# A Hymba decoder layer on one Trainium2 core: the two widest score levels with 66 stationary columns, and one mean square for both value tiles of a GLA head

## The reference

```python
def step(S, inp):                       # per chunk of a head
    q_, k_, v_, g_ = inp
    b = jnp.cumsum(g_, axis=-2)
    diff = b[..., :, None, :] - b[..., None, :, :]
    decay = jnp.exp(jnp.where(causal, diff, -jnp.inf))
    A = jnp.einsum('bhid,bhjd,bhijd->bhij', q_, k_, decay)
    o_intra = jnp.einsum('bhij,bhje->bhie', A, v_)
    o_inter = jnp.einsum('bhid,bhde->bhie', q_ * jnp.exp(b), S)
...
def head_rmsnorm(o, g):                 # over the dv values of a head: 256 in GLA, 128 in HGRN2
    y = o32 * lax.rsqrt(jnp.mean(o32 * o32, axis=-1, keepdims=True) + EPS)
```

## Time and profile before

| | |
|---|---|
| median of three runs | 916.29 us (915.92 to 916.40) |
| the profiled execution | 916.32 us |
| its span in the profile | 914.60 us |
| PE busy | 899.2 us, 98% of the span |
| PEld busy | 746.9 us, 82% |
| DVE busy | 524.7 us, 57% |
| ACT busy | 396.1 us, 43% |
| score matmuls, all levels (L499) | 576 records, 64.5 us of matmul |

### The profile page before, as it was taken

How to read it: one execution, slowest core, us unless ns; L and a number is a source line. 1 busy time by engine, 2 the same in 40 slices (tenths; PEclk the granted TensorE clock), 3 DMA queues, 4 the chain that set the end, 5 groups by cost and what they waited for, 6 DMA issues and landing times.

```text
span 914.6 us, 12106 instructions
## 1 busy us (share of the span) xinstructions
PE 899.2 (98%) x4451; PEld 746.9 (82%) x4451; DVE 524.7 (57%) x838; ACT 396.1 (43%) x536; POOL 64.9 (7%) x95
## 2 busy tenths in 40 slices
PE   8999999999999999999999999999999999999995
PEld 5787888888888888888888888888888888888884
DVE  6632442226365373643457777786875669555756
ACT  6521522224252542525335444644654555434544
POOL 6000001111111100101111100000000000000000
PEclk9999999999999999999999999999999999999998
DMA  7252266667786754646985532123222536865654
GB/s 262 70 160 71 70 173 195 187 198 155 151 161 150 155 157 138 183 138 162 190 191 135 132 95 84 50 69 92 70 70 65 174 107 216 317 224 185 195 173 185
DMA packets 57557, 136.08 MB, mean 149 GB/s; under 512 B 6117, under 2 KB 6153, under 8 KB 56361
## 3 DMA queue, kind: packets, MB, share of 16 engines
q1 hardware_dynamic: 44050, 101.73, 36.0%
q0 software_dynamic: 11264, 33.56, 17.1%
q10 hardware_dynamic: 2200, 0.22, 0.2%
HBM read 131.30 MB, written 37.75 MB: 185 GB/s over the span
## 4 chain that ended last, share of the span: by engine, by line
PE 95%; DVE 2%; ACT 1%; issue 1%; DMA 0%; ACTq 0%; DVEq 0%
PE main L454 67%; PE main L657 7%; PE sc L499 6%; PE sc L657 4%; PE st L657 2%; PE po L657 2%; PE po L523 2%; PE st L510 1%; PE po L526 1%; PE main L558 1%; DVE feat L1143 1%; PE st L488 0%; DVE w_lo L989 0%; PE st L601 0%; ACT fjunk L943 0%
## 5 line engine op out<-in xcount | busy, mean ns | idle before, releaser
L454 PE MATMUL main<-h_hi,w_hi 128*128 128x512 f32 x640 | 258.0, 403 | 0.0
L454 PE MATMUL main<-h_hi,w_lo 128*128 128x512 f32 x640 | 250.2, 391 | 0.0
L454 PE MATMUL main<-h_lo,w_hi 128*128 128x512 f32 x640 | 249.5, 390 | 0.0
L989 DVE TENSOR_TENSOR w_lo<-raw,w_hi 128x1024 fp32r<-128x1024 f32 x115 | 141.0, 1227 | 184.1 <-ACT w_hi L696 183.7
L696 ACT ACTIVATE w_hi<-raw 128x1024 fp32r<-128x1024 f32 x115 | 121.4, 1056 | 241.2 <-PE main L454 221.6
L454 PEld LDWEIGHTS main<-h_hi,w_lo 128*128 128x128 f32 x640 | 120.1, 188 | 26.0
L454 PEld LDWEIGHTS main<-h_hi,w_hi 128*128 128x128 f32 x640 | 120.4, 188 | 22.7
L454 PEld LDWEIGHTS main<-h_lo,w_hi 128*128 128x128 f32 x640 | 120.5, 188 | 22.3
L454 PE MATMUL main<-w_hi,h_hi 128*128 128x512 f32 x256 | 101.9, 398 | 0.6 <-DVE w_lo L989 0.6
L454 PE MATMUL main<-w_hi,h_lo 128*128 128x512 f32 x256 | 99.9, 390 | 0.0
L454 PE MATMUL main<-w_lo,h_hi 128*128 128x512 f32 x256 | 99.8, 390 | 0.0
(11 more groups left out here) (223 smaller groups left out, 1151.5 us busy)
## 6 DMA issues: line engine op xcount, KB each, us to landing
raw<-in_w_in SPq DMA_DIRECT2D x112, 512.0 KB, 4.2
w_sum<-in_w_out POOLq DMA_DIRECT2D x48, 512.0 KB, 5.1
w_sum<-w_sum POOLq DMA_DIRECT2D x16, 512.0 KB, 5.8
raw<-w_sum SPq DMA_DIRECT2D x16, 512.0 KB, 3.3
feat<-w_sum SPq DMA_DIRECT2D x16, 512.0 KB, 3.3
raw<-in_w_out SPq DMA_DIRECT2D x14, 512.0 KB, 3.9
feat<-in_x SPq DMA_DIRECT2D x6, 1024.0 KB, 7.8
feat<-in_w_out SPq DMA_DIRECT2D x10, 512.0 KB, 4.4
```

The source lines that it names most:

```text
L454: mm = pe.matmul(main[c][:, :], a, b, start=(k == 0 and j == 0), stop=(k == KT - 1 and j == 2))
L989: dve.tensor_tensor(w_lo[:, q % SPL, :, :], raw[:, q % RAW, :, :], w_hi[:, q % SPL, :, :], ALU.subtract).then_inc(lo_ok, 1)
```

## The change

Three things change.

1. The keys of level 4 (s = 32) are written packed: 64 a chunk instead of at their own places among 128 (`PACKED`). The stationary operand of level 4 is then 66 columns starting at column 64c, that of level 5 is 66 columns starting at 128c. The last two columns belong to no key of the level and their scores are not read.
2. The scores of level 4 are picked out by two plain copies of 32 partitions x 4 x 32 elements instead of one masked copy; the mask for it goes.
3. In a GLA head the squares of the first tile are kept in f32 in `ex[0]`, the second tile's are added to them in PSUM, and the sum is split into `sq_hi` and `sq_lo` once. PE has one mean square of two matmuls a head, at task 28. `po` is protected by `po_read` instead of by the first mean square. `rstd` and `norm` move from step 6 to step 7 of their engines.

The array part that the built program gives for 66 columns is 128x128.

```diff
...
 
 R_LOG, R_BUP, R_GNW, R_HNW, R_END = 0, 16, 20, 28, 36
 
-KEYS = [P] + [P - s for s in LV]
+KEYS = [P] + [P - s for s in LV[:-2]] + [P // 2 + 2, P // 2 + 2]
+PACKED = NL - 2
 
 T_HQ, T_HF, T_GA = 8, 16, 20
 LN_SHIFT = 2
...
-        maskl = [sb(f"mask{s}", [P, T // 2], U8) for s in LV[:-1]]
+        maskl = [sb(f"mask{s}", [P, T // 2], U8) for s in LV[:-2]]

...
+        sq_first = ex[0][:, :]

...
+        po_read, sq_sum = sem("po_read"), sem("sq_sum")

...
                         if l >= 2:
                             pe.wait_ge(sc_ok, H * NL + (l - 1))
                         w = P if l == 0 else P // 2
-                        m = KEYS[l]
+                        m, at_key = KEYS[l], P // 2 if l == PACKED else P
                         for c in range(NT):
-                            mm = pe.matmul(sc[l % 2][0:m, c * w:(c + 1) * w], kl[l % 2][:, c * P:c * P + m],
+                            mm = pe.matmul(sc[l % 2][0:m, c * w:(c + 1) * w],
+                                           kl[l % 2][:, c * at_key:c * at_key + m],
                                            ql[l % 2][:, c * w:(c + 1) * w], start=True, stop=True)
                         mm.then_inc(sc_ps, 1)
                     return f
...
                         pe.wait_ge(s_ok, X + (xx + 1))
                         if nx == 1:
                             pe.wait_ge(norm_ok, X * 1)
+                        elif xx:
+                            pe.wait_ge(po_read, H + 1)
                         for c in range(NT):
                             cs = slice(c * P, (c + 1) * P)
                             mm = pe.matmul(po[:, cs], vst[vs(xx)][:, c, :], att[:, cs], start=True, stop=(c == 0))
...
                         mm.then_inc(o_ps, 1)
                     return f
 
-                def meansq(xx):
-                    def f():
-                        pe.wait_ge(sq_cut, X + (xx + 1))
-                        ms = ms_bank(nx)
-                        pe.matmul(ms[:, :], ones_r[:, :], sq_hi, start=(xx == 0), stop=False)
-                        mm = pe.matmul(ms[:, :], ones_r[:, :], sq_lo[:, :], start=False, stop=(xx == nx - 1))
-                        if xx == nx - 1:
-                            mm.then_inc(ms_ps, 1)
-                    return f
+                def meansq():
+                    pe.wait_ge(sq_cut, H + 1)
+                    ms = ms_bank(nx)
+                    pe.matmul(ms[:, :], ones_r[:, :], sq_hi, start=True, stop=False)
+                    pe.matmul(ms[:, :], ones_r[:, :], sq_lo[:, :], start=False, stop=True).then_inc(ms_ps, 1)
 
                 def vs(xx):
                     return xx if nx == 2 else at["slot"]
...
                 for xx in range(nx):
                     todo.setdefault(at["U"][xx], []).append(update(xx))
                     todo.setdefault(at["O"][xx], []).append(outputs(xx))
-                    todo.setdefault(at["M"][xx], []).append(meansq(xx))
+                todo.setdefault(at["M"], []).append(meansq)
                 return todo
 
 
...
-            gla_at = dict(slot=0, T=7, L=[9, 11, 12, 14, 15, 17], U=[13, 22], O=[19, 24], M=[22, 27])
+            gla_at = dict(slot=0, T=7, L=[9, 11, 12, 14, 15, 17], U=[13, 22], O=[19, 24], M=28)

...
-                    at = dict(slot=u, T=z, L=[z + q for q in (1, 3, 5, 7, 8, 9)], U=[z + 3], O=[z + 10], M=[z + 14])
+                    at = dict(slot=u, T=z, L=[z + q for q in (1, 3, 5, 7, 8, 9)], U=[z + 3], O=[z + 10], M=z + 14)

...
                     def f():
                         act.wait_ge(o_ps, X + (xx + 1))
                         act.activation(feat[:, q_tile + xx, :], po[:, :], ACT.Copy)
-                        act.activation(sq_hi, po[:, :], ACT.Square).then_inc(o_ok, 1)
-                        act.wait_ge(o_ok, X + (xx + 1))
+                        if nx == 2 and xx == 0:
+                            act.activation(sq_first, po[:, :], ACT.Square).then_inc(po_read, 1)
+                            return
+                        if nx == 1:
+                            act.activation(sq_hi, po[:, :], ACT.Square).then_inc(o_ok, 1)
+                            act.wait_ge(o_ok, H + 1)
                         act.activation(po[:, :], po[:, :], ACT.Square).then_inc(sq_ok, 1)
+                        if nx == 2:
+                            act.wait_ge(sq_sum, H + 1)
+                            act.activation(sq_hi, po[:, :], ACT.Copy).then_inc(o_ok, 1)
                     return f
 
                 def rstd():
...
                 h = head(H, H * 2, 2, 0, H * 2)
                 lv = h["level"]
                 return {0: [h["early"], h["values"]], 1: [lv(1), h["keys"], lv(2)], 2: [lv(3), lv(4), lv(5)],
-                        4: [h["take"](0)], 5: [h["take"](1)], 6: [h["rstd"]]}
+                        4: [h["take"](0)], 5: [h["take"](1)], 7: [h["rstd"]]}
 
             with act.Fori(0, 2) as i:
                 group(i * 2 + G_C, gla_steps(i * 2), store(lambda c: i * 4 + (T_HQ + c), SCALE))
...
                     _, qh = halves(q, s)
                     ek, eq = halves(ex[EXL[l]][:, :], s)
                     keys, _ = halves(kl[l % 2][:, :], s)
+                    if l == PACKED:
+                        keys = kl[l % 2][:, 0:T // 2].rearrange("p (b s) -> p b s", s=s)
                     dve.tensor_tensor(keys, kh, ek, ALU.mult)
                     dve.tensor_tensor(ql[l % 2][:, 0:T // 2].rearrange("p (b s) -> p b s", s=s), qh, eq,
                                       ALU.mult).then_inc(lvl_ok, 1)
...
                             att[:, :].rearrange("p (c n) -> p c n", c=NT),
                             mask0[:, :].rearrange("p (o n) -> p o n", o=1).to_broadcast([P, NT, P]),
                             sc[0][:, :].rearrange("p (c n) -> p c n", c=NT)).then_inc(sc_ok, 1)
-                    elif l < NL - 1:
+                    elif l == PACKED:
+                        s = LV[l - 1]
+                        for b in range(2):
+                            to = att[2 * b * s:(2 * b + 1) * s, :].rearrange("p (c n) -> p c n", c=NT)
+                            got = sc[l % 2][b * s:(b + 1) * s, 0:T // 2].rearrange("p (c n) -> p c n", c=NT)
+                            mm = dve.tensor_copy(to[:, :, (2 * b + 1) * s:(2 * b + 2) * s],
+                                                 got[:, :, b * s:(b + 1) * s])
+                        mm.then_inc(sc_ok, 1)
+                    elif l < PACKED:
                         s, m = LV[l - 1], KEYS[l]
                         _, a = halves(att[0:m, :], s)
                         got = sc[l % 2][0:m, 0:T // 2].rearrange("p (b s) -> p b s", s=s)
...
                                                      op0=ALU.mult, op1=ALU.add).then_inc(s_step if c == 1 else s_ok, 1)
                     return f
 
-                def cut(xx):
-
-                    def f():
-                        dve.wait_ge(sq_ok, X + (xx + 1))
-                        dve.tensor_tensor(sq_lo[:, :], po[:, :], sq_hi, ALU.subtract).then_inc(sq_cut, 1)
-                    return f
+                def cut():
+
+                    dve.wait_ge(sq_ok, H + 1)
+                    if nx == 2:
+                        dve.tensor_tensor(po[:, :], po[:, :], sq_first, ALU.add).then_inc(sq_sum, 1)
+                        dve.wait_ge(o_ok, H + 1)
+                        dve.wait_ge(sq_sum, H + 1)
+                    dve.tensor_tensor(sq_lo[:, :], po[:, :], sq_hi, ALU.subtract).then_inc(sq_cut, 1)
 
                 def norm():
                     dve.wait_ge(rstd_ok, H + 1)
...
                 ar, sl, cp = h["arg"], h["scale"], h["scores"]
                 return {0: [h["args"], h["ends"], h["early"]], 1: [sl(1), ar(3), cp(0), sl(2), ar(4)],
                         2: [cp(1), sl(3), ar(5), cp(2), sl(4), h["states"](0), cp(3), sl(5)],
-                        3: [cp(4), cp(5)], 4: [h["cut"](0)], 5: [h["states"](1), h["cut"](1)], 6: [h["norm"]]}
+                        3: [cp(4), cp(5)], 5: [h["states"](1), h["cut"]], 7: [h["norm"]]}
 
             with dve.Fori(0, 2) as i:
                 group(i * 2 + G_C, gla_steps(i * 2), lambda c: None)
...
-                                   + [f for x in nxt for f in (x["ends"], x["early"])] + [h["cut"](0)])
+                                   + [f for x in nxt for f in (x["ends"], x["early"])] + [h["cut"]])

...
```

## The result

The changed kernel takes 909.21 us (median of six runs, 909.15 to 910.70) against 916.21 (915.92 to 916.40): ratio 0.9923, interval 0.9913 to 0.9933. The forecast was 909.3. Its profiled execution took 909.15 us with a span of 907.3, 7.3 us shorter than before.

The account below looks back on a forecast made before the run. PE's instruction stream was taken to bound the kernel; 2.0 (level 4) + 3.1 (level 5) + 1.9 (mean square) = 7.0 us off the 914.60 span gives 907.6, or 909.3 as a whole; range 908.2 to 912.0.

Parts of the forecast that it names:

- What bounds the kernel: Whole kernel: PE busy 899.2 of 914.60 us; only time taken from its stream, or waits imposed on it, count.
- Part 1, level 4: Level-4 score matmuls, 96 to 66 columns: extra 0.71 to 0.54 us a head, 12 heads, 2.0 us saved.
- the dear end of 0.60: Level-4 groups: upper estimate of the extra per 66-column group, 0.60 us, taken from the 64-column group's matmuls.
- The 62 ns rule: Score matmuls: microcode may spend about 62 ns on each; extra about 0.02 us higher, both levels together 0.5 us dearer.
- Part 2, level 5: Level-5 score matmuls, 64 to 66 columns: standstill goes, extra 0.80 to 0.54 us a head, 12 heads, 3.1 us saved.
- The mixed evidence: Level 5: 96-column loads aren't late, supporting a 64-wide standstill; the low-rank product's 32-column loads show no idle time, against it.
- Part 3: GLA mean square: one pair of matmuls less, 0.47 us in each of four heads, 1.9 us saved; margin 1.8 us.
- Part 4: Level-4 scores on VectorE: two copies occupy 0.42 us against 0.33; 0.34 us of HGRN2 cover remains, cost nil.
- Rival 2: HGRN2 outputs: slow small copies make PE wait, 0.35 us in each of seven heads, 2.5 us: 911.8; chance 10%.
- Rival 1: Levels 4 and 5: the standstill stays at 66 columns, both cost about 0.81 us: 915.7; chance 8%.
- Rival 3: 66-column loads not pulled ahead of running matmuls, each pair losing some 0.08 us, 15 us: 924, slower; chance 2%.
- The range: Whole kernel time: 908.2 to 912.0 us, upper end set to take in rival 2; 80% on the forecast.

Follow-up runs that it names:

- the filling: Changed kernel with level 4 alone undone (96 columns), plus twelve idle transposes of the identity in TensorE's 1.75 us start-up wait: 911.17 us.
- four-copy run: Changed kernel with four more 32x128 VectorE copies, results unused, ahead of the two of level 4 in each head: 916.19 us.

## Why the prediction was right

It said 909.3 and 909.21 came, and the mechanism is the one that it gave. That the two agree to 0.1 us is in part luck: the matmul stream gained 7.14 us instead of 7.0, and the start and the end of the kernel, which the sum put at nothing, moved by +0.48 and -0.36 in the profiled execution. Step by step:

- **What bounds the kernel.** Right. All three gains are PE time taken out of the stream, and they arrive in the total, but for 0.36 us lost on VectorE behind the last matmul.
- **Part 1, level 4:** costed at 2.0 us, measured 2.1 by the extra (0.71 to 0.54) and 2.0 by the times (911.17, with the filling, against 909.21). Going on from 112 and 96 columns in a straight line was sound; the dear end of 0.60 was far off, because it was taken from a group with the defect inside, as the text said.
- **The 62 ns rule** of the Trainium skill ("TensorE: Matmul & The Clock Gate", Back-to-back issue gap): the mean extra came out at 0.54 and the 65-column one at 0.53, without the 0.02 on top. The row was the better guide. It speaks against the rule only if each of the eight recorded pairs counts as a matmul; the kernel issues four, 0.12 us apart, and counted so the rule asks for nothing here.
- **Part 2, level 5:** costed at 3.1, measured 3.2. The mixed evidence is now sorted: the 32-column loads that spoke against it are fp32r, and f32 loads of 32 columns do stand still. The rule of the Trainium skill ("TensorEngine Tiling (Array Packing)", Key Properties), that changing the tiling mode drains TensorE, fits the f32 groups (0.35 us before the loads, once for two joined groups), and not the fp32r ones, which change at no cost. The measurement decides: here only the f32 groups pay, all of which are also short.
- **Part 3:** 1.9 costed, 1.9 measured by the medians (1.7 without the executions of the longer kind). The chain was put 0.2 us too long; margin 1.8 forecast, 2.03 measured. ScalarE's table load and first store are in time too, no PE wait appears at the next group.
- **Part 4:** the outcome was right and the size of a term off. An instruction was taken to occupy its duration less 0.1, as its neighbours do; the 32x128 copies last 0.28 us and occupy 0.29, so the pair takes 0.58 and not 0.42. Of 0.34 us of forecast cover 0.26 to 0.34 were left in seven heads, since the level-5 copy followed the scan more closely than before (1.26 us from start to start instead of 1.35) and gave a part back. That two errors cancelled is luck. Rival 2 was nearer than its text made it look. By the text's own rule two copies of 0.7 us occupy 1.2, 0.87 more than the old one, against 0.44 of cover: 0.43 in each of seven heads, 3.0 us and not 2.5, which lies outside the range. The four-copy run shows that the wait takes effect at once in those seven.
- **Rival 1** is the kernel with 64 columns at both levels, forecast 915.7, measured 915.96. It didn't happen because the 66-column form isn't of that kind. **Rival 3** found nothing: the loads are pulled ahead as always.
- **The range** held. That one of six runs took 910.7 fits the fall of the clock at 30 us, which the prediction didn't know of; that run has no trace.

## What to carry to other kernels

Where small f32 matmuls are threaded into a stream of large ones, look at the first weight load of each group: here a stationary operand of 64 or 32 columns cost 0.24 to 0.27 us a group more than one of 65, and padding it to 65 or 66 with columns nobody reads took that away. Compare a form with its wider neighbour instead of trusting that fewer columns are cheaper. And when a change pulls a saturated engine forward, count what is left between its waits and their releasers afterwards: here 0.87 us became 0.26, and a second small addition would be felt at full price.

## What the runs showed of the hardware

- Groups of f32 matmuls with 64 or 32 stationary columns (64 moving) between fp32r ones over the whole array: 0.35 us without a load on the way in, and 0.24 to 0.27 us more a group than at 65 columns; 65 and 66: no such pause. A single f32 transposition on 36 rows: the same 0.35. fp32r matmuls with 64 or 32 stationary columns (512 moving): none. Groups that follow each other in the same form pay once.
- TensorE's clock fell from 2.4 to 1.2 GHz for 3.4 us at 30 us into the kernel in two of fourteen traces, behind a wait of 1.75 us in a start-up with many short waits; the stretch before it looked the same in an execution where it didn't fall. Such executions took some 1.75 us longer.
- VectorE copies of 32x128 out of PSUM that start at changing partitions (0 and 32) ran at 0.29 us each without overlap, while a 64x256 copy of 0.42 us overlaps with its follower by 0.08 and a 128x2 copy of 0.16 us by 0.09.
